# The decay chain of a gated linear scan, in three steps with weight splits between them

## What is computed

```
r_f, r_b, q, k, v, ...  = split(h @ w_in)                      # h: 256 latent rows, 256 context rows
la = log_sigmoid(r @ w_d + b_d) / 16                           # forward and backward decays, 4 heads x 128
# per direction and head, over tokens t:
S_t = diag(exp(la_t)) S_{t-1} + k_t^T v_t ;  o_t = q_t S_t
# the context is scanned first (s = 1 in the kernel), its last S starts the latent scan (s = 0)
br_a = ((a_b * short_conv(a_c * a_x)) * silu(a_z)) @ w_br_conv  # branch a, runs beside the scans
```

## Time and profile before

| | us |
|---|---|
| median of 3 runs | 2122.3 |
| lowest and highest | 2122.16, 2123.07 |
| profiled execution, its own time | 2121.59 |
| its span, first to last instruction | 2119.7 |
| PE busy in it | 2065.7 (97%) |
| DVE, ACT busy | 1354.1 (64%), 953.0 (45%) |
| granted TensorE clock, mean | 0.993 |

### The profile page before, as it was taken

The page is one execution under the profiler, slowest core; times in us unless marked ns, Lnnn a source line. Parts: engine busy times, 40 slices in busy tenths (PEclk is TensorE's granted clock), DMA queues, the critical chain, the costliest instruction groups (busy, mean ns, idle before and its releaser), DMA issues.

```text
span 2119.7 us, 31505 instructions
## 1 busy us (share of the span) xinstructions
PE 2065.7 (97%) x12154; PEld 1791.2 (84%) x12154; DVE 1354.1 (64%) x2375; ACT 953.0 (45%) x1564; POOL 135.9 (6%) x140
## 2 busy tenths in 40 slices
PE   7999999999999999999999999999999989999998
PEld 6779998778999888888888778888878889888997
DVE  6756667666877428568444555868555588475665
ACT  4645555554555424353323463223244554445443
POOL 1000000000110100000100001111110000100100
PEclk9999999999999999999999999999999999999999
DMA  8436666424555432212222204534234234251553
GB/s 251 150 128 230 229 216 199 159 100 150 179 180 190 148 100 70 70 60 80 70 97 83 70 21 149 181 130 145 95 118 160 100 119 149 91 179 52 193 175 129
DMA packets 79300, 285.81 MB, mean 135 GB/s; under 512 B 8800, under 2 KB 9452, under 8 KB 79152
## 3 DMA queue, kind: packets, MB, share of 16 engines
q1 hardware_dynamic: 70848, 256.93, 35.9%
q10 hardware_dynamic: 6272, 19.51, 2.5%
q0 software_dynamic: 2032, 7.35, 1.3%
HBM read 277.92 MB, written 5.83 MB: 134 GB/s over the span
## 4 chain that ended last, share of the span: by engine, by line
PE 83%; DVE 9%; ACT 4%; issue 2%; DMA 2%; POOL 0%; DVEq 0%; ACTq 0%; SPq 0%
PE pb L977 16%; PE pb L979 16%; PE pb L978 16%; PE pb L990 6%; PE pb L992 6%; PE pb L991 6%; DVE SPL L1986 3%; PE pb L996 2%; PE pb L1141 2%; PE pb L1142 2%; PE pb L1143 2%; PE pb L1213 2%; PE pb L1316 2%; PE pb L1297 2%; ACT SPH L1437 1%
## 5 line engine op out<-in xcount | busy, mean ns | idle before, releaser
L1986 DVE TENSOR_TENSOR SPL<-RAW,SPH 128x1024 fp32r<-128x1024 f32 x460 | 560.1, 1232 | 402.6 <-ACT SPH L1437 379.1
L977 PE MATMUL pb<-HTH,SPH 128*128 128x256 f32 (+1 forms) x2008 | 646.5, 322 | 11.8 <-DVE SPL L1986 6.1
L979 PE MATMUL pb<-HTH,SPL 128*128 128x256 f32 (+1 forms) x2008 | 638.3, 318 | 0.0
L978 PE MATMUL pb<-HTL,SPH 128*128 128x256 f32 (+1 forms) x2008 | 638.1, 318 | 0.0
L1437 ACT ACTIVATE SPH<-RAW 128x1024 fp32r<-128x1024 f32 x462 | 478.4, 1051 | 247.8 <-PE pb L979 120.5
L977 PEld LDWEIGHTS pb<-HTH,SPH 128*128 128x128 f32 x2008 | 382.6, 191 | 40.7 <-issue 7.3
L978 PEld LDWEIGHTS pb<-HTL,SPH 128*128 128x128 f32 x2008 | 382.7, 191 | 26.4
L979 PEld LDWEIGHTS pb<-HTH,SPL 128*128 128x128 f32 x2008 | 382.5, 190 | 26.0
L990 PE MATMUL pb<-SPH,HTH 128*128 128x512 f32 x640 | 255.5, 399 | 0.5 <-DVE QNB L2411 0.5
L991 PE MATMUL pb<-SPH,HTL 128*128 128x512 f32 x640 | 251.1, 392 | 0.0
L992 PE MATMUL pb<-SPL,HTH 128*128 128x512 f32 x640 | 251.1, 392 | 0.0
(11 more groups left out here) (275 smaller groups left out, 2529.4 us busy)
## 6 DMA issues: line engine op xcount, KB each, us to landing
RAW<-in_w_up SPq DMA_DIRECT2D x88, 512.0 KB, 4.5
RAW<-in_wa SPq DMA_DIRECT2D x64, 512.0 KB, 3.2
RAW<-in_w_in SPq DMA_DIRECT2D x48, 512.0 KB, 4.4
RAW<-in_wmg SPq DMA_DIRECT2D x48, 512.0 KB, 3.3
RAW<-in_wbr SPq DMA_DIRECT2D x48, 512.0 KB, 3.3
RAW<-in_w_down SPq DMA_DIRECT2D x44, 512.0 KB, 4.7
RAW<-in_w_ada SPq DMA_DIRECT2D x24, 512.0 KB, 4.8
ARAW<-in_w_ada ACTq DMA_DIRECT2D x24, 512.0 KB, 4.3
```

The lines of the kernel that those rows point to most:

```text
L977: T.matmul(o, wh[:, kt, :], xh[:, kt, n0:n1], start=kt == 0, stop=False)
L978: T.matmul(o, wh[:, kt, :], xl[:, kt, n0:n1], start=False, stop=False)
L979: m = T.matmul(o, wl[:, kt, :], xh[:, kt, n0:n1], start=False, stop=kt == 7)
L1986: W.tensor_tensor(lo, raw, hi.bitcast(F32), SUB).then_inc(*dve.tick(s["lo_dve"], ("u", u)))
```

## The change

The chain becomes three steps in place of two. `gdec2` keeps the MAX half of the clamps and the first Exp. `gln` takes the MIN half and, as before, Ln and the combination. The last Exp is a step of its own, `gexp`. `GAPS` puts scan steps between them: 1 and 2 in layer 0, 2 and 3 in layer 1. `PC` falls from (8, 17) to (6, 11), and one scan step is put between `ginit` and `gprod -1`. In layer 0, `KEYS` now starts the scan under the values' second group: `gdec` after its first weight, `gdec2` after its second, `gln` after its third, `gexp` and `ginit` after its fourth, ahead of the copies `gv`. For that the values' first group takes PSUM banks 0 to 3 and the second 4 to 7, and the first `gdec` takes 0 to 3. In layer 1 `KEYS` begins (2, 2, ...) in place of (2, 1, ...).

```diff
-IC, PC = (4, 5), (8, 17)
-KEYS = ((0,) * 8, (2, 1, 1, 2, 2, 2, 2, 1))
+IC, PC = (4, 5), (6, 11)
+GAPS = ((1, 2), (2, 3))
+KEYS = ((0, 0, 0, 0, 1, 1, 1, 2), (2, 2, 1, 2, 2, 2, 2, 1))
...
             for i in range(4):
-                self.take(ring, ("gd", l, s, i))
+                self.take(LO4 if s > l else ring, ("gd", l, s, i))
                 self.add("gdec", l, s, i)
             yield
             self.add("gdec2", l, s)
+            yield GAPS[l][0]
+            self.add("gln", l, s)
             for i in range(4):
                 self.give(("gd", l, s, i))
-            yield
-            self.add("gln", l, s)
+            yield GAPS[l][1]
+            self.add("gexp", l, s)
             yield PC[l]
             self.add("ginit", l, s)
             if full:
+                yield 1
                 for hp in range(2):
                     self.take(ring, ("gp", l, s, -1, hp))
                 self.add("gprod", l, s, -1)
...
-            for _ in self.group_n(("gv", l, g), f"wgv{l}", g, (0, 1, 2, 3), LO4 if last else ALL8, H):
+            for _ in self.group_n(("gv", l, g), f"wgv{l}", g, (0, 1, 2, 3), HI4 if g and not last else LO4, H):
...
+    def gexp(l, st):
         for d in range(2):
             et = sb["ET"][:, d, :]
             act.wait_ge(s["gla_dve"], ("la", l, st, d))
...
     def gdec2(l, st):
         k.past(dve, f"gla{l}{st}", SCAN)
         spilled(dve, k, l)
-        for op, o in ((MAX, sb["E4"]), (MIN, sb["ET"][:, :, :].rearrange("p d (i n) -> p (d i) n", i=2))):
...
+        for i in range(4):
+            dve.wait_ge(mm, ("gd", l, st, i))
+            for hh in range(2):
+                c = slice(hh * 256, hh * 256 + 256)
+                W.tensor_scalar(sb["E4"][:, i, c], k.P(("gd", l, st, i))[:, c], par("b_dec", l * 8 + i * 2 + hh),
+                                LOWEST, ADD, MAX).then_inc(
+                    *dve.tick(s["gla_dve"], *([("z", l, st, i // 2)] if hh and i % 2 else [])))
 
     def gln(l, st):
+        for i in range(4):
+            name = ("gd", l, st, i)
+            for hh in range(2):
+                c = slice(hh * 256, hh * 256 + 256)
+                W.tensor_scalar(sb["ET"][:, i // 2, i % 2 * 512 + hh * 256:i % 2 * 512 + hh * 256 + 256],
+                                k.P(name)[:, c], par("b_dec", l * 8 + i * 2 + hh), LOWEST, ADD, MIN).then_inc(
+                    *(dve.free(*k.read(name)) if hh else dve.tick(s["gla_dve"])))
         for d in range(2):
             et = sb["ET"][:, d, :]
             dve.wait_ge(s["gla_act"], ("ln", l, st, d))
```

More of the change, by code:

```diff
@@ L1879, in scalar_program @@
             "y": y, "y_turn": y_turn, "up": up, "tables": tables, "spill_ctx": spill_ctx, "spill_x": spill_x,
-            "spill2": spill2, "wdec": wdec, "rank": rank, "gk": gk, "gq": gq, "gv": gv, "gdec2": gdec2, "gln": gln,
+            "spill2": spill2, "wdec": wdec, "rank": rank, "gk": gk, "gq": gq, "gv": gv, "gdec2": gdec2, "gln": gln, "gexp": gexp,
             "ginit": ginit, "gwiden": gwiden,
@@ L2246, in gdec2 @@
         spilled(dve, k, l)
-        for op, o in ((MAX, sb["E4"]), (MIN, sb["ET"][:, :, :].rearrange("p d (i n) -> p (d i) n", i=2))):
[L2248 to L2256, removed]
-    def gln(l, st):
+        for i in range(4):
[5 more added lines that the diff above has]
+                    *dve.tick(s["gla_dve"], *([("z", l, st, i // 2)] if hh and i % 2 else [])))
+    def gln(l, st):
+        for i in range(4):
[5 more added lines that the diff above has]
+                    *(dve.free(*k.read(name)) if hh else dve.tick(s["gla_dve"])))
         for d in range(2):
```

## The result

| | us |
|---|---|
| before, median of 10 runs beside it | 2122.33 |
| after, median of 10 runs | 2126.49 (2124.08 to 2130.12) |
| ratio | 1.0023 (95% interval 1.0014 to 1.0031) |
| profiled execution of after, span | 2125.92, 2124.1 |
| granted clock, mean | 0.992 |

A forecast was written before the change was run, and what follows sets the result against it. PE, at work 97% of the span, bounds the kernel; only its waits can be won. Terms -2.8 + 3.4 + 0.7 - 0.4 = +0.9 us gave 2123 (2120 to 2126, chance 0.58); 8-in-10 range 2117 to 2128.

The forecast's parts named there:

- term 2: Layer 0, s = 0: wait at `gprod 0` grows from 1.4 to 4.3 us, short waits go, clock 1.2: +3.4 us.
- term 4: Layer 1, s = 0: the 6.1 us wait becomes 3.1 and 3.5, with 1.4 at `gprod 0`: -0.4 us.
- the first rival: Splits come in time, layer 0, s = 0, wait no longer: 2113, or 2117 at one place; chance 0.18.
- the chain's length: Layer 1, s = 0: from MAX's start (M), last Exp ends at M + 11.0, low half at M + 13.4.
- M + 18.0: Layer 0, s = 0: W0, needed by `gprod 0`, comes 18.0 us after M, the start of MAX.
- Term 1: Layer 0, s = 1: 2.8 us wait and 0.75 of clock go, 0.8 comes at later `gprod`: -2.8 us.
- M = T + 13.5: Layer 0, s = 0: MAX begins (M) 13.5 us after T, the end of c, ft 3 on PE.
- Term 3: Layer 1, s = 1: last Exp, splits and copies end 1.0 us later, 0.4 to spare: +0.7 us.
- the second (the clock falls at every new wait, 2127): Waits of 3 to 4 us bring as long a low clock as 6.1 did: +4.8 us, 2127; chance 0.18.
- The third: Layer 0, s = 1: values' copies too late, 2.8 us wait moves ahead: +3.7 us, 2126; chance 0.06.

The follow-up runs named there:

- gnorm_narrow: After, but in layer 0, s = 1, POOL scales 8 columns of each head instead of 256; 2125.2 us, ratio to before 1.0020.
- gwiden_behind_split: After, with one scan step between `gprod j` and `gwiden j` in layer 1, s = 0, and one less behind; 2125.1 us, ratio to before 1.0017.
- l1_half_later: After, with one more scan step ahead of `ginit` in layer 1, s = 0; 2123.1 us, ratio to before 1.0005.
- combined: Layer 0 as in l0_split_between; layer 1, s = 0, chain in five steps, s = 1 as before; 2117.1 us, ratio to before 0.9981.
- l0_split_between: After, with layer 0, s = 0, gaps of two steps between `gdec2` and `gln`, thirteen between `gexp` and `ginit`; 2122.0 us, ratio to before 1.0005.
- l0_init_later: After, with four more scan steps between `gexp` and `ginit` in layer 0, s = 0; 2121.5 us, ratio to before 0.9998.
- combined2: combined, with `gexp` two steps later in layer 0, s = 0, and `ginit` three earlier in layer 1, s = 0; 2113.1 us, ratio to before 0.9959.
- new_layer1: After, but layer 0 in the order of before; 2124.4 us, ratio to before 1.0011.

## Why the prediction was right where it was, and wrong where it was

**The number.** The range held, the forecast did not come close: +0.9 us was added up, and the stretches say +5.1. The median is 0.5 us outside the narrower 2120 to 2126. Two errors of the same sign, one in term 2 and one in term 4, fell within a range that was made wide for other reasons (the clock, the first rival); that part is luck. In the sum itself the bounds of the four terms add up to -2.3 and +4.1, not to -4.6 and +4.1; 2120 to 2126 fits the right sum.

**What bounds, and the chain's length.** Right. MAX to W0 in layer 0, s = 0, was 18.0 us (916.06 to 934.04), the M + 18.0 of the working.

**Term 1 (-2.8).** Right: no wait at `gprod 0`, and 0.22 and 0.33 us at two later ones in place of the 0.5 and 0.3. With the clock, -3.0.

**Term 2 (+3.4).** The mechanism was right, the size some 1.6 us short (4.64 - 1.38 + 0.85 - 0.7 + 1.65 = 5.1 by the waits and the clock, 4.9 by the stretch with term 1 taken off). The wait was 4.64, but the 0.85 us for the low half behind the combination were not in the working, and the clock took 1.65 and not 1.2; the two short waits went. The step that failed is "M = T + 13.5": MAX began 14.9 us after ACT had turned to c, ft 3 (901.14 to 916.06). That step priced `ba_x` at 3.6 us from a place where POOL was idle, and put it right behind `gnorm`, which starts POOL. The five instructions took 5.05 us (910.97 to 916.02), 1.5 more, and gnorm_narrow shows that they are POOL's. The clock's part varies from run to run: behind the same wait it was low for 6.8 us in after and 3.4 in gwiden_behind_split. The working of layer 0 by stretches: +1.9 against +0.6.

**Term 3 (+0.7).** Right: 0.57 us of wait at the values' second group, 0.85 in the stretch.

**Term 4 (-0.4).** For the chain it was right: waits of 3.0 and 1.9 on SPL. The second was to be 3.5, the 1.4 at `gprod 0` did not come, and the clock was low between the waits instead (0.74 and 0.71 by the windows), so PE came later by itself; the sum is the same. (In gnorm_narrow, where the clock was low there in one piece of 6.8 us, the second wait is 1.0 and `gprod 0` waits 1.0.) l1_half_later, which keeps this chain and gives the `gprod` back their order, shows it by itself: 209.49 against 209.69, -0.2. The step that failed is its last sentence: "The rest of the scan has the same DVE work between `gprod` and keeps its 1.1." The work was the same, but the half weight by which the `gprod` moved put ACT's high half behind KC, and the 1.1 became 3.4. That is +2.3 us, nearly half of the 5.1 by the stretches. The order of the two lists, ACT's and DVE's, showed it, and I had looked at it for the chain alone. On the table load the trace of after agrees with that of before: 1.28 us (1714.24), and the Exp begins 0.02 later, without the drain that the Trainium skill, ScalarE: Activation LUTs, What ACT_TABLE_LOAD costs, puts on top.

**The rivals.** The time came out near that of the second (the clock falls at every new wait, 2127), but not for its reason: the clock's part beyond what was taken is about 0.5 us. The first did not happen: DVE's row was as long as worked out in layer 1 and longer in layer 0. The third did not either: the values' copies came in time.

## What to carry to other kernels

When a change shifts a periodic stage by half a step, write out one period of every engine's list again: the same work between two deadlines says nothing on which copy now stands behind which wait. Where a wait is removed from the bounding engine, ask what that engine reaches next and who makes it: here each mended place uncovered the next (`gprod 0`, a low half, a high half). Layer 0's stretch was 2.3 us shorter than before with the first mended, 1.5 with the second as well, and 4.6 with all three. A split between two parts of a chain helped here only where both its halves, ACT's and DVE's, came out from behind the chain.

## What the hardware showed that I had not expected

- One DVE instruction with both inputs in SBUF took 2.00 us in place of 0.48 beside two POOL instructions of 1.96 us each, and 0.48 with these cut short (gnorm_narrow). It shows as a longer instruction, not as idle time with a releaser.
- PE's clock does not go by a wait's length alone. It fell behind the single waits of 6.1 and 2.8 us of before, of 4.6 (after), 4.2 (gnorm_narrow), 2.5 (combined) and 2.3 (l0_split_between), but not behind the one of 2.7 in l0_init_later, nor through the six of 0.1 to 1.3 us in layer 1 of combined2. The window row of that run (length, busy us (matmuls), granted clock, DMA share, GB/s):

```profile
1700.00:1790.00 90.00, 85.46 (x705) 1.00 0.41 139
```

- At 531 us, behind a wait of 1.8 us that every kernel here has, the clock falls in some executions and not in others. First combined2, then before:

```profile
531.50:534.90 3.40, 3.40 (x10) 0.50 0.75 257
```

```profile
531.50:534.90 3.40, 3.40 (x22) 1.00 0.86 252
```

Such places are part of the scatter from run to run: in the ten runs of after the mean granted clock falls from 0.995 in the fastest (2124.08) to 0.991 in the slowest (2130.12). Where the clock was low in the runs without a trace is not shown, and in other kernels, as new_layer1, time and mean clock do not go together.
